# The half step of attention between the two contexts' steps, in a two-layer hybrid encoder step on one core

## The reference, cut to what matters

```python
def step(Sm, inp):
    r_t, w_t, k_t, v_t, kk_t, a_t = inp
    sa = jnp.einsum('bhij,bhj->bhi', Sm, kk_t)
    Sm = (Sm * w_t[:, :, None, :] - sa[..., None] * (kk_t * a_t)[:, :, None, :]
          + v_t[..., None] * k_t[:, :, None, :])
    return Sm, jnp.einsum('bhij,bhj->bhi', Sm, r_t)
...
s = (jnp.einsum('bqhc,bkc->bhqk', qlb, ckv)
     + jnp.einsum('bqhr,bkr->bhqk', qrb, kr)).astype(jnp.float32) * MLA_SCALE
s = jnp.where(key_chunk[None, :] <= q_chunk[:, None], s, -jnp.inf)
pr = jax.nn.softmax(s, axis=-1).astype(ckv.dtype)
return jnp.einsum('bhqk,bkc->bqhc', pr, ckv)
```

## Time and profile before

| what | us |
|---|---|
| median of 3 runs | 1833.26 |
| the runs | 1831.84 to 1834.72 |
| the profiled execution | 1831.97 |
| its span | 1829.9 |
| PE busy in the span | 1759.7 |
| DVE busy | 1132.5 |
| ACT busy | 869.2 |
| POOL busy | 239.2 |

### The profile page before, as it was taken

One profiled execution on the slowest core, in us unless ns is written; L12 is line 12 of the kernel. 1 busy time (PEld: TensorE's weight loads), 2 busy tenths in 40 slices (PEclk: granted clock), 3 DMA queues, 4 the chain that ended last, 5 costly groups with the idle time before them and its releaser, 6 DMA issues.

```text
span 1829.9 us, 38018 instructions
## 1 busy us (share of the span) xinstructions
PE 1759.7 (96%) x16242; PEld 1640.5 (90%) x16242; DVE 1132.5 (62%) x1976; ACT 869.2 (48%) x1589; POOL 239.2 (13%) x210
## 2 busy tenths in 40 slices
PE   7989898999999999999999899999999999999997
PEld 7976777999799999999999677789987999999997
DVE  7786676544478666665367966666444776656653
ACT  5454556553356444444345455555434654444432
POOL 0010000300014222221100100011000332222201
PEclk9999999999999999999999999999999999999999
DMA  6100001461022322223231000133510222222221
GB/s 244 68 8 1 4 27 56 164 219 59 24 89 74 105 93 93 93 93 104 73 139 47 9 3 3 37 140 120 191 53 29 93 93 93 93 93 93 93 93 61
DMA packets 38758, 149.53 MB, mean 82 GB/s; under 512 B 4416, under 2 KB 4576, under 8 KB 36928
## 3 DMA queue, kind: packets, MB, share of 16 engines
q1 hardware_dynamic: 36288, 131.05, 21.0%
q0 software_dynamic: 2304, 16.06, 2.3%
HBM read 139.68 MB, written 7.41 MB: 80 GB/s over the span
## 4 chain that ended last, share of the span: by engine, by line
PE 81%; DVE 11%; ACT 5%; issue 2%; DMA 0%; DVEq 0%; ACTq 0%; SPq 0%
PE PS L829 59%; PE PS L1019 13%; PE PS L1047 5%; PE PS L1038 2%; DVE wL L1950 1%; DVE wL L1946 1%; ACT wH L1441 1%; DVE hbL L2419 1%; DVE stat L2313 1%; DVE xT L1976 1%; ACT hb L1441 1%; DVE hL L1964 1%; ACT aP L1441 1%; PE PS L1295 0%; ACT L1441 0%
## 5 line engine op out<-in xcount | busy, mean ns | idle before, releaser
L1441 ACT ACTIVATE wH<-ring 128x1024 fp32r<-128x1024 f32 (+1 forms) x294 | 261.4, 891 | 331.7 <-PE PS L829 268.2
L829 PE MATMUL PS<-hH,wH 128*128 128x272 f32 x1760 | 382.4, 299 | 13.2 <-DVE hL L1959 8.1
L829 PE MATMUL PS<-hH,wL 128*128 128x272 f32 x1760 | 366.3, 289 | 0.0
L829 PE MATMUL PS<-hL,wH 128*128 128x272 f32 x1760 | 365.3, 289 | 0.0
L1950 DVE TENSOR_TENSOR wL<-ring,wH 128x1024 fp32r<-128x1024 f32 x182 | 230.7, 1269 | 184.5 <-ACT wH L1441 183.6
L829 PEld LDWEIGHTS PS<-hH,wH 128*128 128x128 f32 x1760 | 278.4, 189 | 28.4 <-issue 12.6
L829 PEld LDWEIGHTS PS<-hH,wL 128*128 128x128 f32 x1760 | 277.9, 189 | 0.0
L829 PEld LDWEIGHTS PS<-hL,wH 128*128 128x128 f32 x1760 | 276.3, 189 | 0.0
L1019 PE MATMUL PS<-hbH,wH 128*128 128x272 f32 x784 | 227.1, 290 | 1.2 <-DVE hT L2475 0.9
L1019 PE MATMUL PS<-hbH,wL 128*128 128x272 f32 x784 | 227.0, 289 | 0.0
L1019 PE MATMUL PS<-hbL,wH 128*128 128x272 f32 x784 | 225.6, 288 | 0.0
(11 more groups left out here) (374 smaller groups left out, 3522.9 us busy)
## 6 DMA issues: line engine op xcount, KB each, us to landing
ring<-wall SPq DMA_DIRECT2D x238, 512.0 KB, 3.3
lw<-lw_in POOLq DMA_DIRECT2D x2, 1856.0 KB, 7.5
xT<-x_in SPq DMA_DIRECT2D x4, 544.0 KB, 6.0
y_out<-hT SPq DMA_DIRECT2D x8, 272.0 KB, 2.1
mem<-mem_in POOLq DMA_DIRECT2D x2, 1024.0 KB, 5.1
mks<-mks_in POOLq DMA_DIRECT2D x2, 1024.0 KB, 5.7
mvs<-mvs_in POOLq DMA_DIRECT2D x2, 1024.0 KB, 8.7
memk_out<-mkp POOLq DMA_DIRECT2D x2, 1024.0 KB, 6.2
```

The source lines that it names most:

```text
L829: return e.matmul(out, lhsT=a, rhs=b, start=start, stop=stop)
L1441: return e.activation(out, in_, f, **kw)
```

## The change

Within a pair the first half step of attention now stands between the two steps, and the second half step, where there is one, after the second step. A pair "rra" becomes "rar", a pair "rraa" becomes "rara". The last pair, with one step and two half steps, stays "raa". The steps, the half steps and the order among each kind stay as they are, on all three engines.

```diff
     pairs, left = (len(REC_STEPS) - ALONE + 1) // 2, ATT_STEPS - order.count("a")
     for j in range(pairs):
-        order += "r" * min(2, len(REC_STEPS) - order.count("r")) + "a" * (left * (j + 1) // pairs - left * j // pairs)
+        steps, halves = min(2, len(REC_STEPS) - order.count("r")), left * (j + 1) // pairs - left * j // pairs
+        order += "ra" + "r" * (steps - 1) + "a" * (halves - 1)
     return order
```

## The result

The changed kernel takes **1856.5 us**, median of 6 runs (1848.6 to 1865.3), beside 1833.1 (1831.8 to 1834.7) of the kernel before: a ratio of 1.013, 95% interval 1.0105 to 1.0156. It is slower by 23 us; predicted were 1837.1 and a range that ended at 1845. Times of the same kernel shift a little from one occasion to the next (the kernel before: 1831.5 to 1833.7 us), and the changed kernel itself was run on this occasion only. The profiled execution took 1853.8 us with a span of 1851.7, against 1832.0 and 1829.9.

A forecast was written before the change was run, and what follows sets the result against it. It took TensorE (PE), busy 96% of the span, as the bound. Its terms, -3.6 + 2.8 - 1.5 + 1.4 + 2.8, gave +1.9 us a layer, +3.8 in all, hence 1837.1 us; range 1829 to 1845.

The forecast's parts named there:

- The signs that it named for its mechanism: In the paired stretch: hT, rs waits under 0.3 us; 0.5 to 2 before three crosses; lw 2.5 or more; TK 0.8.
- Nothing: PE's other single waits, 0.9 us or less each: no cost; if cover fails, each can grow 0.46 to 0.68 us.
- the clock: PE idle ahead of pair 35's weighing lets the clock fall: about 1843.1 us, sharing chance 0.10 with full switch costs.
- Removed waits: Between neighbouring half steps of attention: waits for ACT hT, DVE rs and part of lw go, -3.6 us a layer.
- Switches: In 21 pairs PE goes once more from recurrence to attention and back, 0.2 us each, two thirds counted: +2.8 a layer.
- Crosses meeting: After pairs 7, 9 and 11 the two lanes' cross products become neighbours and wait for DVE's mask: +2.8 us a layer.
- Second half: From pair 25 on DVE starts rotation and normalising earlier and PE's waits for P shrink: -1.5 us a layer.
- Tail: Pairs 35 and 36: solve of group 3 and its blocks become neighbours, ACT's copy lies open: +1.4 us a layer.

The follow-up runs named there:

- y3: The changed kernel with pairs 7, 9, 11, 16 and 34 to 36 back in the old order; 1835.5 us, ratio 1.0019.
- y4: The kernel before with only pairs 1, 8, 10, 12, 13, 22 and 25 changed; 1827.3 us, ratio 0.9973.
- y1: The kernel before with only pairs 7, 9 and 11 changed; 1842.7 us, ratio 1.0067.
- z1: The kernel before with only pairs 34 to 36 changed, plus seven constant matmuls where PE waits for ACT there; 1836.0 us, ratio 1.0018.
- z3: The changed kernel with pair 16 alone back in the old order; 1842.9 us, ratio 1.0064.
- y2: The kernel before with only pairs 34, 35 and 36 changed; 1842.6 us, ratio 1.0063.

## Why the prediction was wrong

Wrong in size, right in sign: slower had the largest chance, 0.42, but the time lies 11 us above the range. The signs that it named for its mechanism came (hT and rs gone, waits of 1.07, 1.67 and 0.62 us at lane 0's crosses, 2.57 for lw, though near 298 us and not 292, and 0.70 for TK ahead of the last blocks). At equal clock the changed kernel stands at 1843.5, 6 us above the forecast and still inside the range: two steps failed, the term called "Nothing", which adds 3.6 us, and above all the clock, which no term of the sum has and which adds 11 to 13. By its own steps, at full clock and for one layer (stretches whose window has clock 1.00):

- **Removed waits, -3.6.** Right: hT and rs are gone, lw has only the wait in pair 35. From tokens(0) to tokens(2) y3, which has the removal and neither a meeting nor solve's wait, has 3.0 us less idle time of PE a layer.
- **Switches, +2.8.** Too small, inside the bounds: PE's busy time in y3 grows by 1.5 us ahead of tokens(2) and 2.3 behind it, 3.8 a layer at full clock. That is 0.20 for each of the 19 pairs of y3 that now go back and forth once more, just the price it had. In y4, with seven such pairs, it grows by 1.0 and 0.3, which is 0.18 a pair. The third that was to hide in waits did not hide. The drain that the Trainium skill's page names (TensorEngine Tiling (Array Packing), Key Properties) would fit this; no run here switches tiles and nothing else, so that the cause of the growth is not shown.
- **Crosses meeting, +2.8.** Right in place, a little small: y1's layer 1 takes 61.6 us from tokens(0) to tokens(2) at clock 1.00 against 58.2, +3.4. The cross of pair 10 came at 206.33, 1.46 later, predicted 1.5. That of pair 8 came no later (198.69 for 198.70), where +0.5 was predicted.
- **Second half, -1.5.** Wrong: y3 is 0.7 us longer from tokens(2) on, though two removed waits lie in it, and its crosses and merges wait for P 1.7 us in 3 waits where they waited 1.5 in 2. The gain that came (0.9 in y4) is that of the removed waits.
- **Tail, +1.4.** Near: z1's layer takes 30.9 us at clock 1.00 from the norm's first sums to its second against 29.2, +1.7 with its fills; the changed kernel's own layer 1 takes 31.2 there at clock 1.00, +2.0.
- **Nothing, PE's other single waits.** This failed. "What they wait for moves by as much as they do" isn't so for solve(1), because in pair 16 A moves ahead of the merge whose copies solve needs, while solve's own place doesn't gain cover. z3 shows it at 1.8 us a layer, more than the 0.46 to 0.68 by which the prediction let one such wait grow if its cover failed. The prediction had looked at meetings of two crosses and of solve(3) with blocks(3) and not at the same pattern, merge then solve, in lane 1.
- **The clock.** This failed most. It was one clause in a rival, with a chance of 0.10 shared with the switches, for one place only, and with the argument that the clock in layer 1 had been 1.00 throughout. That a stretch whose waits are 1.1 us at most keeps its clock says nothing of one with waits of 1.7 to 2.6. The sum priced a wait at its own length; here the order's 10 us brought another 11 to 13 with them.

A bound could have been had from rows of before: the clock of 0.99 in layer 0 was one fall of 3.4 us at 268.6, behind PE's wait of 0.67 at 266.98. Layer 1 has the same wait (at 1168.67) and no such fall, so that wait alone does not decide it, but it was the sign that the clock can fall within the pairs. The prediction itself foresaw four new or longer waits a layer, at three crosses and the weighing. Half of 3.4 us for each of the eight is 14 us, and 1837.1 + 14 is 1851: the upper end of the range belonged there, not at 1845. The measured 1856.5 would have been above it even so.

## What to carry to other kernels

When PE is the bound and a change opens waits of 1 us or more on it, price each at its length and again at half of a stretch at half clock that may follow (3.4 to 31 us long here), and put that into the range. Before moving a turn, list for every step of the chain the last copy it needs, and what stands ahead of that copy on ACT or DVE in the new order; a chain step that becomes the neighbour of its own producer is the price. Undoing just those pairs was not enough here (y3, 0.19% slower than before); the gain came where only those pairs were changed that had a wait to lose (y4, 0.27% faster). A wait that can't be removed can be filled: constant products in it took 6.6 us off the tail's order (y2 to z1), with the first useful product behind the wait no earlier against the work ahead of it.

## What the runs showed of the hardware

- The granted clock goes to 0.5 in or behind waits of 1.2 to 2.6 us on PE (1.21 us ahead of 1186.74 in layer 1 of the changed kernel, with the fall at 1187.8, is the shortest of them in that trace), but not each time: in one execution the wait of 2.57 us ahead of the weighing was followed by 10.2 us at half clock in layer 0, and in layer 1 the same wait by none, as a row of PE's timeline and a window of the changed kernel show. With the fills in y2's tail, 10 executions out of 10 had at most 13 us lost; without them up to 31.

```profile
1213.56 0.32 PE L830 MATMUL PS<-aPTf,av 128*64 128x128 f32 x1 [2.56 <-ACT lw L1442]
```

```profile
1195.50:1226.70 31.20, 26.02 (x487) 21.22 (x483) 14.49 (x47) 15.95 (x40) 0.57 (x1) 1.00 0.05 17
```

- At half clock a stretch can go on while PE is busy: in y2 it lasted 31 us from 289.3 us, with PE busy for 9.20 of the 10 us from 290 to 300 and for all of those from 310 to 320:

```profile
290.00:300.00 10.00, 9.20 (x123) 7.98 (x123) 1.12 (x4) 1.60 (x5) 0.00 (x0) 0.50 0.01 2
310.00:320.00 10.00, 10.00 (x34) 7.27 (x33) 7.33 (x11) 8.18 (x13) 0.00 (x0) 0.50 0.24 70
```

- Executions of one kernel spread with its waits: 1848.6 to 1865.3 us for the changed kernel at a clock of 0.989 to 0.976, 1826.0 to 1829.4 for y4 at 0.995 to 0.997. A spread of 0.9% where another kernel of the same program has 0.2% is itself a sign of the clock.
- A us lost to the clock, by the records, costs 0.64 us of time. That part of what runs at half clock would have been waiting anyway is a likely reason; no run shows it.
